# Two transformer blocks on one core: another order in the first attention, and weights split one chunk further ahead in the paired attention and the third square projection

## The reference

```
h = rms_norm(x, attn_norm_g[0]); x = x + diff_attention(h, ...) # 8 heads, two softmaxes each, their difference
h = rms_norm(x, ffn_norm_g[0]);  x = x + conv_ffn(h, ...)       # 1024 -> 2 x 2816, 3 taps, silu gate, -> 1024
h = rms_norm(x, attn_norm_g[1]); x = x + mla_attention(h, ...)  # latents 384 and 256, 16 heads in 8 pairs
h = rms_norm(x, ffn_norm_g[1]);  x = x + conv_ffn(h, ...)
return rms_norm(x, final_norm_g)
```

## Time and profile before

| | us |
|---|---|
| median of three runs | 1062.94 (1062.31 to 1062.98) |
| the profiled execution | 1061.37 |
| its span, first to last instruction | 1059.6 |
| TensorE busy | 1029.9 |
| VectorE busy | 728.7 |
| ScalarE busy | 572.1 |
| mean granted clock of TensorE | 0.995 |

### The profile page before, as it was taken

How to read it: one execution, slowest core, us unless ns; L and a number is a source line. 1 busy time by engine, 2 the same in 40 slices (tenths; PEclk the granted TensorE clock), 3 DMA queues, 4 the chain that set the end, 5 groups by cost and what they waited for, 6 DMA issues and landing times.

```text
span 1059.6 us, 19997 instructions
## 1 busy us (share of the span) xinstructions
PE 1029.9 (97%) x7892; PEld 989.7 (93%) x7892; DVE 728.7 (69%) x968; ACT 572.1 (54%) x796; POOL 6.6 (1%) x20
## 2 busy tenths in 40 slices
PE   7999999999999999999999999999989999999997
PEld 6999999999999999878889999999988899999996
DVE  6666655557664664867868777777855587777775
ACT  7455565545444433567756555554634565555554
POOL 0000000000000000000000000000020000000000
PEclk9999999999999999999999999999999999999999
DMA  8645665556665455354545656664423375666651
GB/s 295 198 145 173 208 198 165 190 167 196 203 201 193 160 184 209 124 159 133 186 121 155 204 178 178 178 178 124 128 47 86 119 219 160 183 190 191 189 161 76
DMA packets 191266, 178.89 MB, mean 169 GB/s; under 512 B 17444, under 2 KB 169586, under 8 KB 191218
## 3 DMA queue, kind: packets, MB, share of 16 engines
q1 hardware_dynamic: 191218, 178.22, 54.3%
HBM read 177.15 MB, written 1.05 MB: 168 GB/s over the span
## 4 chain that ended last, share of the span: by engine, by line
PE 88%; DVE 7%; ACT 3%; issue 1%; DMA 1%; SPq 0%; DVEq 0%; ACTq 0%
PE psum L609 24%; PE psum L611 23%; PE psum L610 23%; PE psum L616 4%; PE psum L617 4%; PE psum L618 4%; DVE whl L1701 2%; ACT whl L1220 2%; PE psum L950 1%; DVE stat L2072 1%; DMA raw<-ffn_w_up 1%; PE psum L949 1%; DMA x_rows<-x 0%; PE psum L934 0%; ACT hT L1252 0%
## 5 line engine op out<-in xcount | busy, mean ns | idle before, releaser
L609 PE MATMUL psum<-hT,whl 128*128 128x256 f32 x1392 | 394.7, 284 | 0.7 <-DVE hT L1776 0.6
L611 PE MATMUL psum<-hT,whl 128*128 128x256 f32 x1392 | 393.8, 283 | 0.0
L610 PE MATMUL psum<-hT,whl 128*128 128x256 f32 x1392 | 393.8, 283 | 0.0
L1701 DVE TENSOR_TENSOR whl<-raw,whl 128x2048 fp32r<-128x2048 f32 (+2 forms) x145 | 297.4, 2056 | 93.7 <-ACT whl L1220 93.5
L1220 ACT ACTIVATE whl<-raw 128x2048 fp32r<-128x2048 f32 (+2 forms) x145 | 248.8, 1717 | 119.4 <-DMA raw<-w_ff 70.1
L609 PEld LDWEIGHTS psum<-hT,whl 128*128 128x128 f32 x1392 | 266.7, 192 | 2.1 <-issue 0.8
L610 PEld LDWEIGHTS psum<-hT,whl 128*128 128x128 f32 x1392 | 266.8, 192 | 0.8
L611 PEld LDWEIGHTS psum<-hT,whl 128*128 128x128 f32 x1392 | 266.7, 192 | 0.0
L609 PE MATMUL psum<-lat,whl 128*128 128x256 f32 (+1 forms) x512 | 146.4, 286 | 5.1 <-DVE whl L1701 5.1
L610 PE MATMUL psum<-lat,whl 128*128 128x256 f32 (+1 forms) x512 | 145.5, 284 | 0.0
L611 PE MATMUL psum<-lat,whl 128*128 128x256 f32 (+1 forms) x512 | 145.4, 284 | 0.0
(11 more groups left out here) (246 smaller groups left out, 1383.8 us busy)
## 6 DMA issues: line engine op xcount, KB each, us to landing
raw<-w_ff SPq DMA_DIRECT2D x32, 1024.0 KB, 5.5
raw<-w_in SPq DMA_DIRECT2D x24, 1024.0 KB, 5.2
raw<-ffn_w_up SPq DMA_DIRECT2D x44, 512.0 KB, 5.1
q_sb<-ffn_w_up SPq DMA_DIRECT2D x44, 512.0 KB, 5.1
raw<-da_w_qkv SPq DMA_DIRECT2D x12, 1024.0 KB, 5.1
q_sb<-ffn_w_down SPq DMA_DIRECT2D x22, 512.0 KB, 3.6
raw<-ffn_w_down SPq DMA_DIRECT2D x22, 512.0 KB, 3.7
raw<-w_proj_a SPq DMA_DIRECT2D x4, 1024.0 KB, 5.1
```

The source lines that it names most:

```text
L609: mm(dst, weight(n, 0, cols, kt, c0, m), hi, start=start, stop=False, skip_group_check=True)
L610: mm(dst, weight(n, 0, cols, kt, c0, m), lo, start=False, stop=False, skip_group_check=True)
L611: return mm(dst, weight(n, 1, cols, kt, c0, m), hi, start=False, stop=stop, skip_group_check=True)
L1701: tt(whl[:, slot, 1, 0:w], landing(n)[:, 0:w], whl[:, slot, 0, 0:w].bitcast(F32), ALU.subtract).then_inc(lo_ready, 1)
```

## The change

In the first attention the output turns 0 and 1 swap their banks, `da_outputs(0)` and `(1)` come earlier and apart, and with them `round_outputs` and `split_outputs`; `sum_x(QKV, 1)`, its mean, deviation and reciprocal come later, and `normalise_x` is done in one piece ahead of `split_lo(n + 5)`. One call of Sqrt on a dummy is gone. `ffn` sums squares by `add_pair` where the next stage is not QKV. The turned reciprocal of the latents goes to `px` instead of `py`. In the paired attention and behind it both halves of a chunk stand one chunk further ahead, and `square_stage` gets a parameter `lead`, which is 3 for `N_WO2`.

```diff
-            return (bank[3], bank[1], up[0], up[1])[c]
+            return (bank[1], bank[3], up[0], up[1])[c]
...
 (TensorE, first attention)
             turn_rows(0, 0)
+            rows(1, 0, (1,))
+            turn_rows(0, 1)
+            rows(1, 1, (0,))
             pe.wait_ge(std_ready, sum(SUMS[:QKV]) + 1)
             mean(QKV, 1)
-            rows(1, 0, (1,))
-            turn_rows(0, 1)
-            rows(1, 1)
+            rows(1, 1, (1,))
...
             turn_rows(3, 1)
+            da_outputs(0)
             rows(5, 1, (0,), early)
             da_scores(4)
+            da_outputs(1)
             rows(5, 1, (0,), late)
-            da_outputs(0)
-            da_outputs(1)
...
 (TensorE, latents)
-                    pe.wait_ge(kpe_ready, 1)
-                    turn_reciprocal(1)
+                    pe.wait_ge(lat_std, 1)
+                    turn_reciprocal(1, px)
...
-                    pe.wait_ge(lat_std, 1)
+                    pe.wait_ge(r_read, 1)
...
 (ScalarE, square_stage)
-                split_hi(n0 + LEAD)
+                if lead == LEAD:
+                    split_hi(n0 + LEAD)
...
                     round_x(c, gain)
                     square_x(c)
-                    if c < 3:
-                        split_hi(n + 1 + LEAD)
+                    if lead > LEAD:
+                        split_hi(n + lead)
+                    elif c < 3:
+                        split_hi(n + 1 + lead)
...
 (ScalarE, first attention)
             take_columns(0, 0)
-            deviation(QKV, 1)
             take_columns(0, 1)
             split_hi(n + 3)
             take_rows(1, 0)
+            deviation(QKV, 1)
             take_rows(1, 1)
...
             output_deviation(0, 2)
+            split_hi(n + 11)
             take_columns(3, 1)
+            round_outputs(0)
             fn(eps[:, 3:4], eps[:, 0:1], ACT.Exp)
-            split_hi(n + 11)
             exponentials(4, 4, up)
+            round_outputs(1)
             take_rows(5, 0)
-            round_outputs(0)
-            round_outputs(1)
...
-            fn(eps[:, 1:2], eps[:, 0:1], ACT.Sqrt)
             output_squares(2)
             output_deviation(2, 1)
             take_turned(7)
+            round_outputs(2)
             split_hi(n + 15)
-            round_outputs(2)
...
 (ScalarE, paired attention)
+            split_hi(N_UQ + LEAD)
...
-                if proj:
-                    split_hi(N_UQ + c + LEAD)
+                if c < 8:
+                    split_hi(N_UQ + c + LEAD + 1)
...
 (VectorE, square_stage)
-                    if c < 3:
-                        split_lo(n + LEAD)
+                    if c < 3 and lead == LEAD:
+                        split_lo(n + lead)
                     rest_x(k, c, gain)
                     if c > 0:
                         add_pair(k, c)
+                    if c < 3 and lead > LEAD:
+                        split_lo(n + lead)
                 tt(ss[:, 0, :], ss[:, 0, :], ss[:, 1, :], ALU.add).then_inc(ss_ready, 1)
-                split_lo(n0 + 3 + LEAD)
+                split_lo(n0 + 3 + lead)
...
 (both, ffn)
-                split_lo(n0 + 2)
+                if k != FFN1:
+                    split_lo(n0 + 2)
...
 (VectorE, end of ffn)
+                    if k + 1 != QKV and c > 1:
+                        add_pair(k + 1, c - 1)
...
-                    sum_x(k + 1)
+                    add_pair(k + 1, 3)
+                    tt(ss[:, 0, :], ss[:, 0, :], ss[:, 1, :], ALU.add).then_inc(ss_ready, 1)
...
 (VectorE, first attention)
             split_lo(n + 1)
-            sum_x(QKV, 1)
             rope(0, 0)
             rope(0, 1)
             split_lo(n + 2)
-            step.wait(step.mark(reciprocal_deviation(QKV, 1)))
+            sum_x(QKV, 1)
             split_lo(n + 3)
             rope(1, 0)
             rope(1, 1)
+            step.wait(step.mark(reciprocal_deviation(QKV, 1)))
             split_lo(n + 4)
-            normalise_x(range(0, KT // 2))
+            normalise_x()
             split_lo(n + 5)
-            normalise_x(range(KT // 2, KT))
...
             norm_outputs(1)
+            split_lo(n + 11)
             pair_max(4)
-            split_lo(n + 11)
+            split_outputs(0)
             weights(4)
+            split_outputs(1)
             pair_max(5)
-            split_outputs(0)
-            split_outputs(1)
             split_lo(n + 12)
...
-            split_lo(n + 14)
             split_outputs(2)
             take_outputs(3)
+            split_lo(n + 14)
...
 (VectorE, paired attention)
+            split_lo(N_UQ + LEAD)
...
                     pair_max(DA_HEADS + c - 1)
-                    split_lo(N_UQ + c - 1 + LEAD)
+                    if c < 8:
+                        split_lo(N_UQ + c + LEAD)
...
             pair_rest(5)
+            split_lo(N_WO2 + LEAD)
             pair_outputs(7)
...
-            square_stage(N_WO2, FFN1, column("ffn_norm_g_2", KT))
+            square_stage(N_WO2, FFN1, column("ffn_norm_g_2", KT), LEAD + 1)
```

More of the change, by code:

```diff
@@ L672, in mean, with turn_reciprocal @@
                 last.then_inc(mean_ready, 1)
-            def turn_reciprocal(half):
+            def turn_reciprocal(half, bank):
                 for t in range(TT):
-                    last = nc.tensor.transpose(py[:, 1, t * P:(t + 1) * P], rstd[:, half, t * P:(t + 1) * P], ident)
+                    last = nc.tensor.transpose(bank[:, 1, t * P:(t + 1) * P], rstd[:, half, t * P:(t + 1) * P], ident)
                 last.then_inc(r_turned, 1)
@@ L975, in da_outputs @@
                 pe.wait_ge(of_ready, c + 1)
-                pe.wait_ge(*((turned_read, 8), (rows_read, 10), (prob_ready, 8), (prob_ready, 8))[c])
+                pe.wait_ge(*((rows_read, 10), (turned_read, 8), (prob_ready, 8), (prob_ready, 8))[c])
                 for b in range(2):
@@ L1355, in _, with square_stage @@
                 fn(mT[:, bass.ds(i * 2, 2), 0, :], t_dve[:, 0, :, :], ACT.Copy).then_inc(m_hi, 1)
-            def square_stage(n0, gain):
-                split_hi(n0 + LEAD)
+            def square_stage(n0, gain, lead=LEAD):
+                if lead == LEAD:
+                    split_hi(n0 + LEAD)
                 for c in range(4):
@@ L1406, in unit @@
                         split(1)
-                split_hi(n0 + 2)
+                if k != FFN1:
+                    split_hi(n0 + 2)
                 deviation(k)
@@ L1464, in take_reciprocal @@
                 act.wait_ge(r_turned, which)
[L1465 removed]
+                fn(r_tok[:, at:at + TT], px[:, 1, :].rearrange("p (t q) -> p t q", t=TT)[:, :, 0],
                    ACT.Copy).then_inc(r_read, 1)
@@ L1661, in _ @@
             pair_turned_out(7)
-            square_stage(N_WO2, column("ffn_norm_g_2", KT))
+            square_stage(N_WO2, column("ffn_norm_g_2", KT), LEAD + 1)
             ffn(2, N_FFN1, FB, FFN1)
@@ L1929, in _, with square_stage @@
                    ALU.subtract).then_inc(m_ready, 1)
-            def square_stage(n0, k, gain):
+            def square_stage(n0, k, gain, lead=LEAD):
                 for c in range(4):
@@ L2037, in take_deviation, with normalise_x @@
                 ts(r_da[:, 2, :], r_da[:, 1, :], DA_SCALE, None, ALU.mult).then_inc(r_ready, 1)
-            def normalise_x(kts):
-                for kt in kts:
+            def normalise_x():
+                for kt in range(KT):
                     stt(xT[:, kt, :], xT[:, kt, :], gain("norm_final_g", kt), rstd[:, 1, :], ALU.mult, ALU.mult)
```

## The result

The changed kernel takes 1052.7 us (median of 4 runs, 1051.98 to 1053.47) against 1062.96 (1062.31 to 1063.06): 10.3 us less, a ratio of 0.9901 with a 95% interval of 0.9889 to 0.9913. The profiled execution took 1052.46 us, its span is 1050.7. The forecast was 1053.5, with a range of 1048.7 to 1057.0.

The account below looks back on a forecast made before the run. TensorE's work, busy 1029.9 of 1059.6 us, was taken as the bound, so only idle time or lost clock could be won. The terms sum to 9.4 us, 1061.37 to 1052.0, or 1053.5 as a median; range 1048.7 to 1057.

Parts of the forecast that it names:

- part 1: First attention, position turn: the 2.01 us wait for k_sb goes, a 0.7 wait at the mean comes; gain 1.3 us.
- part 2: First attention, x normalised in one piece: the waits of 0.3 (prob) and 0.8 (attn) go; gain 1.1 us.
- Part 3: Output turns 0 and 1: of a 1.15 us wait for mT, 0.6 won; VectorE is the next limit, 0.3 waits.
- Part 4: Output turns 2 and 3: idle of 2.26 us becomes 0.5, gain 1.75, and 1.5 more from the kept clock.
- the rival that rested on it: Output turns 2 and 3: a drain behind the table load makes it 1.3 us worse, 1054.8; chance 0.02.
- Part 5: End of the first convolution stage: sum_x becomes pair sums and the mean comes earlier; gain 0.2 us.
- Part 6: Latent turn: turn_reciprocal no longer waits for kpe_ready, so the hf wait goes; gain 0.6 us.
- part 7: Paired attention, weights one chunk further ahead: whl waits go, prob waits of 0.9 and 0.35 come; gain 5.45 us.
- Part 8: Third square projection: adds of x 6.2 us apart, a 3.2 us hT stall and half clock; loss 3.1 us.
- the lock: Third square projection: VectorE's low half waits for ScalarE's high half of the same step, 6.2 us per step.
- first rival: Third square projection: the square stage does not lock, 4.7 us better, 1048.8; chance 0.10.
- second rival: The clock does not come back: waits of 0.5 and 0.9 still end at 1.2 GHz, 3.0 us worse, 1056.5; chance 0.12.

Follow-up runs that it names:

- The single edit: The kernel before with only the position-turn and normalising edits of the first attention: 1057.63 us, ratio 0.9960.
- The later mean: The changed kernel with third-square low halves a step later, plus the first attention's mean behind all of rows(1, 1) and its deviation behind take_rows(1, 1): 1045.91 us.
- The fill: The kernel before with 4 unread matmuls in each of the idles of 2.26 and 2.37 us: 1059.38 us, ratio 0.9968.
- the kernel without it: The changed kernel with VectorE's low halves in the third square projection one step later, ahead of the rests: 1047.76 us, ratio 0.9863.
- the fill: The changed kernel with 6 unread matmuls in its 3.34 us stall for hT: 1051.16 us, against 1052.41 for the changed kernel beside it.

## Why the prediction was right, point by point

**Parts 1 and 2** held in their waits: those that went are the named ones, the one that came (0.77 for `ss`) was put at 0.7. The single edit gave 2.23 of 2.4. The sum is closer than its terms: from the first product to the scores of head 0 it is 25.87 us, before 26.89, so part 1 gave 1.0 of 1.3, and from there to the last turn 39.65, before 40.87, so part 2 gave 1.2 of 1.1. The later mean shows why part 1 is short: the new wait with its row of 0.77 costs 1.2.

**Part 3** held: 0.65, and the limit is the one that was named. The 0.3 at both turns is there, though no idle row shows it; the turns of heads 5 and 6 start 0.43 and 0.44 behind the product before them instead of 0.22, as `weights` ends at 519.53 and 524.70:

```profile
524.31 0.39 PE L943 MATMUL psum<-v_sb,attnT 128*128 128x128 f32 x2
524.75 0.55 PE L934 MATMUL psum<-const,attn 128*128 128x128 f32 x3
```

The wait of 0.27 for `prob` at 512.15 was not foreseen.

**Part 4** held: 0.51 for 0.5, and 1.4 to 1.5 for the clock. The fill shows that 1.5 is a cost of TensorE's idle time itself, apart from the 1.75 of waiting. The two rows of ScalarE behind the squares:

```profile
529.00 1.28 ACT L1493 ACT_TABLE_LOAD   x1
530.30 0.30 ACT L1493 ACTIVATE ostat<-ostat,eps 128x4 f32<-128x4 f32 x1
```

The deviation starts 0.02 behind the load of 1.28. The drain that the Trainium skill (page ScalarE: Activation LUTs, section What ACT_TABLE_LOAD costs) puts beside it is not seen at its new place either, and the rival that rested on it did not come.

**Part 5** held, 0.21, and 0.11 with the pair sums and the latent turn alone (first product to mean 310.72 us, before 310.83).

**Part 6** was 0.1 to 0.25 too small, and **part 7** 0.55 too small. This is the term that was mis-sized. By step, forecast and measured: to scores(1) 3.0 and 2.77, to scores(2) 1.4 and 1.19, and from there 1.05 and 2.04. The two `prob` waits are 1.21 and 0.55, not 0.9 and 0.35; what I had too small were the four short waits of 0.43 and 0.2. I priced a wait at its idle row. TensorE in the trace of before, the turn of the probabilities and the projection behind it:

```profile
802.79 0.82 PE L934 MATMUL psum<-const,prob 128*128 128x128 f32 x6
...
804.04 0.39 PE L609 MATMUL psum<-lat,whl 128*128 128x256 f32 x1 [0.43 <-DVE whl L1701]
```

The idle of 0.43 is counted from 803.61, the recorded end of the turn. But without a wait the projection does not start there. After the change the turn at 786.72, also of 0.82, is followed by the projection at 787.29, that is 0.57 behind its start and 0.25 ahead of its recorded end. So the wait removed gives back 0.43 + 0.25, and one of 0.2 gives 0.45: the period falls from 6.10 to 5.62. The latent turn (0.85 for 0.62) and the later mean (1.2 for 0.77) show more than the row on other lines, and two waits at head 0 show that the excess is not a fixed one: scores(0) to scores(1) is 6.53 us instead of 6.94, 0.41 for a row of 0.33, and from there to the turn 0.86 instead of 1.71, 0.85 for 0.78. That the end of a matmul in a trace is worked out and not observed is also what the Trainium skill says (page Perfetto Trace Analysis, section Tensor Engine Instruction (MATMUL, LD_WEIGHTS)); the figure of 0.25 is this trace's.

**Part 8** held in each step: adds 6.2 apart (6.20 to 6.27), a stall of 3.34 for 3.2, half clock behind it, and -3.11 for -3.1. Its two pieces are shown apart, the lock as a whole by the kernel without it (4.7 to 4.9, forecast 4.7 in the first rival) and the clock by the fill (1.4, forecast 1.5).

**The rivals.** The square stage did lock. The clock came back in both places. First attention kept its gain. No landing was waited for in the third square projection. All of this is in the trace after.

**What was wrong without harm**: "Shorter idles, of 2.01 us and less, left the clock at 1.00." That was true of one trace. The same idle of 2.01 for `k_sb` is there in six profiles with this stretch unedited. In four the clock stays at 1.00, in two it does not; here the two windows of the kernel with 4 fill matmuls:

```profile
446.00:448.00 2.00, 0.42 (x3) 0.42 (x4) 1.83 (x9) 1.87 (x1) 0.00 (x0) 0.95 0.92 323
448.00:450.00 2.00, 2.00 (x7) 1.67 (x6) 1.97 (x4) 1.07 (x2) 0.00 (x0) 0.50 0.46 176
```

From the first product to the scores of head 0 those two have 28.5 us, before 26.9: it cost 1.6. So what the position turn's edits give is, by this estimate, 2.25 in some executions and 3.9 in others, and some 2.8 on the average if it is 2 in 6. This goes some way to explain the 4.6 of its single run (interval 2.7 to 5.7), not all of it, and the rest stays open. The idle of 1.52 before the last scores, too, was followed by 0.75 and 0.50 once, in the kernel without the lock, and cost 1.7 there (13.66 us to the next wait, 12.00 in the changed kernel):

```profile
816.00:818.00 2.00, 1.16 (x4) 1.10 (x5) 1.65 (x4) 2.00 (x6) 0.00 (x0) 0.75 0.02 7
818.00:820.00 2.00, 2.00 (x9) 1.73 (x8) 0.27 (x1) 1.20 (x1) 0.00 (x0) 0.50 0.96 298
```

Nor is the price of half the clock fixed. In the trace of the position turn's edits the same idle of 2.26 is followed by a longer stretch of it, and the 36 matmuls take 7.10 us, not 5.85 as in three other traces, nor 4.33 as at full clock: 2.8 lost, not 1.5.

```profile
535.46 0.55 PE L609 MATMUL psum<-mT,whl 128*128 128x256 f32 x1 [2.26 <-DVE mT L2110]
...
542.56 0.60 PE L979 MATMUL psum<-const,hf 128*128 128x128 f32 x4
```

Had I given this a chance, part 1 would have been larger, and the chance of the second rival, that waits of 0.5 and 0.9 still end at half clock, would have rested on a range of idles and not on a limit.

**The sum**: 9.4 forecast, 10.0 by the traces, 10.3 and 10.0 by the medians of two measurements. The four kernels with one group of edits each add up to 11.9 by their medians; each is uncertain by about 1, so no interaction can be read from that.

## What to carry to other kernels

- Price a removed wait of TensorE by the distance from start to start, against the same pair of instructions where it does not wait, not by its idle row: where a wait was removed whole, the row understated it by 0.07 to 0.44 us, which matters most where the waits are short and repeated. A wait that is added costs more than its row in the same way.
- Doing a half of the weights a step earlier is only free if the engine that makes the first half has made it a step before. Look for two engines that then wait for each other within one step; a step later on the second engine alone was worth 4.7 us here.
- A filler shows what a lost clock costs, but its own length must be known first: a fill that overruns its gap looks like a null result. How far it overran is read from a landmark just ahead of it, as two traces can be half a microsecond and more apart there.

## What the runs showed of the hardware that I had not expected

- An idle of 2.01 us is followed by half clock in 2 of 6 profiles, one of 1.52 in 1 of the 13 profiles that have it; one of 1.71 in none of 6; those of 2.26, 2.37 and 3.34 us in every profile that has them (4, 4 and 3). It costs 1.4 to 1.7 us each time but one, and 2.8 that once.
- A plain float32 matmul of 256 columns (L1068) is recorded as two of 0.226 us at full clock, 0.45 in all; one of fp32r halves of the same size (L609) takes 0.12 (36 in 4.33).
- The same code up to the first attention takes 438.2 to 440.1 us from profile to profile, which is as much as one part of this change.
